# A two-layer hybrid decoder step: coarse and fine GLA products together, attention of the prompt in pairs of query blocks

## The reference, cut to what matters

```python
def layer(x, ...):
    h = rmsnorm(x, g_pre)
    (c_x, c_b, c_c, c_z, g_q, g_k, g_v, g_lr, g_z,
     s_q, s_k, s_v, s_z, m_q, m_z) = split_cols(h @ w_in)
    # A: short gated conv
    # B: GLA, 4 heads of 64: S_t = diag(a_t) S_{t-1} + k_t^T v_t, o_t = q_t S_t
    # C: sliding-window attention, window 128, rotary, a learned sink per head
    # D: cross-attention into 256 memory tokens
    mix = jnp.concatenate([a_out, b_out, c_out, d_out], axis=-1) @ w_out
    return x + rmsnorm(mix, g_post)

def memory_attention(q, mk, mv):
    s = jnp.einsum('blhd,bmhd->bhlm', q, mk) * (hd ** -0.5)
    p = jax.nn.softmax(s, axis=-1)
    return jnp.einsum('bhlm,bmhd->blhd', p, mv)
```

## Time and profile before

| | |
|---|---|
| median of 3 runs | 2365.94 us (2365.74 to 2366.8) |
| profiled execution | 2365.44 us |
| its span, first to last instruction | 2363.6 us |
| TensorE busy, matmuls | 2325.7 us, 14532 records |
| TensorE busy, weight loads | 1845.8 us |
| VectorE busy | 1369.8 us |
| ScalarE busy | 918.0 us |
| GpSimd busy | 108.2 us |
| mean granted clock of TensorE | 0.999 |

### The profile page before, as it was taken

How to read it: one execution, slowest core, us unless ns; L and a number is a source line. 1 busy time by engine, 2 the same in 40 slices (tenths; PEclk the granted TensorE clock), 3 DMA queues, 4 the chain that set the end, 5 groups by cost and what they waited for, 6 DMA issues and landing times.

```text
span 2363.6 us, 40015 instructions
## 1 busy us (share of the span) xinstructions
PE 2325.7 (98%) x14532; PEld 1845.8 (78%) x14532; DVE 1369.8 (58%) x3346; ACT 918.0 (39%) x2111; POOL 108.2 (5%) x179
## 2 busy tenths in 40 slices
PE   8999999999999999999999999999999999999998
PEld 4677777787788888878877777777878888787877
DVE  4566746565456765655536767365644676555443
ACT  4444324344434333344434543153434443233331
POOL 1000000001000000000000000000100000000000
PEclk9999999999999999999999999999999999999999
DMA  7110212244210122223331111132340113142132
GB/s 242 28 54 21 62 36 63 58 157 131 71 46 20 42 65 75 67 65 125 135 90 36 28 45 46 50 94 92 131 122 20 53 29 74 25 108 60 47 117 80
DMA packets 230557, 172.12 MB, mean 73 GB/s; under 512 B 56886, under 2 KB 206908, under 8 KB 230332
## 3 DMA queue, kind: packets, MB, share of 16 engines
q1 hardware_dynamic: 226100, 154.78, 22.8%
q10 hardware_dynamic: 4264, 14.78, 1.8%
HBM read 136.60 MB, written 21.93 MB: 67 GB/s over the span
## 4 chain that ended last, share of the span: by engine, by line
PE 95%; DVE 2%; issue 1%; ACT 1%; DMA 1%; ACTq 0%; SPq 0%; DVEq 0%; POOL 0%; POOLq 0%
PE bank L1725 53%; PE bank L2749 16%; PE bank L1820 3%; PE bank L2020 3%; PE bank L1978 3%; PE bank L1965 2%; PE bank L1804 2%; PE bank L1168 1%; PE bank L1797 1%; PE bank L1866 1%; PE bank L1962 1%; PE bank L2765 1%; PE bank L1860 1%; PE bank L1772 1%; PE bank L2010 1%
## 5 line engine op out<-in xcount | busy, mean ns | idle before, releaser
L1725 PE MATMUL bank<-h_hi,w_hi 128*128 128x512 f32 (+3 forms) x2160 | 484.5, 361 | 11.3 <-DVEq L2290 4.1
L1725 PE MATMUL bank<-h_lo,w_hi 128*128 128x512 f32 (+3 forms) x2160 | 488.7, 363 | 1.8
L1725 PE MATMUL bank<-h_hi,w_lo 128*128 128x512 f32 (+2 forms) x2080 | 468.2, 362 | 1.5
L1725 PEld LDWEIGHTS bank<-h_hi,w_hi 128*128 128x128 f32 (+1 forms) x2160 | 354.0, 186 | 89.4 <-issue 31.6
L1725 PEld LDWEIGHTS bank<-h_lo,w_hi 128*128 128x128 f32 (+1 forms) x2160 | 351.1, 185 | 73.6 <-issue 15.4
L1725 PEld LDWEIGHTS bank<-h_hi,w_lo 128*128 128x128 f32 x2080 | 343.5, 188 | 69.0 <-issue 16.2
L2749 PE MATMUL bank<-scr_r,tb_r 128*128 128x512 f32 x816 | 195.1, 395 | 2.1 <-ACT scr_r L2089 1.6
L2749 PEld LDWEIGHTS bank<-scr_r,tb_r 128*128 128x128 f32 x816 | 151.7, 188 | 36.8 <-issue 3.4
L2070 ACT ACTIVATE tb<-bank 128x512 f32<-128x512 f32 (+1 forms) x140 | 71.2, 508 | 192.8 <-PE bank L1725 186.6
L2229 ACT ACTIVATE scr<-bank 128x512 f32<-128x512 f32 x132 | 77.9, 590 | 170.3 <-PE bank L1978 169.0
L2428 DVE COPY_PREDICATED scr<-level_mask,bank 128x128 f32<-128x128 uint8 (+1 forms) x332 | 116.7, 351 | 45.6 <-PE bank L1820 26.9
(11 more groups left out here) (289 smaller groups left out, 3117.3 us busy)
## 6 DMA issues: line engine op xcount, KB each, us to landing
w_raw<-in_w_in SPq DMA_DIRECT2D x96, 512.0 KB, 3.7
out<-scr SPq DMA_DIRECT2D x32, 512.0 KB, 2.7
scr<-in_w_out SPq DMA_DIRECT2D x16, 512.0 KB, 4.9
w_raw<-in_w_out SPq DMA_DIRECT2D x16, 512.0 KB, 3.5
scr<-in_x_prompt SPq DMA_DIRECT2D x16, 512.0 KB, 3.7
scr<-out SPq DMA_DIRECT2D x16, 512.0 KB, 3.3
rot<-out ACTq DMA_DIRECT2D x12, 512.0 KB, 3.7
mix_t<-in_x_prompt ACTq DMA_DIRECT2D x8, 512.0 KB, 13.8
```

Source lines behind the costliest of these rows:

```text
L1725: m = mm(bank[b][0:m_w, 0:c1 - c0], w[:, slot, k, 0:m_w], h[:, k, c0:c1], start=it["piece"] == 0 and k == 0, stop=it["piece"] == 2 and k = ...
```

## The change

Two things. In B, `gla_g` and `gla_f` of a chunk are placed as one (both sets of banks must be free), `gla_t` stands ahead of them; the level-64 products write all 128 rows; and `gla_o` does the two products with `a` first where fine products, a score or a value visit stood last on TensorE. In C and D, items cover two blocks (`PAIRS` = 2 per step): score writes 512 columns of banks 6 and 7, `turn` fills banks 2 and 3, `value` one bank (4 for the first pair, 5 for the second). C now scales and masks in place in PSUM, and its banks too are held until the exponential. There is one buffer for the probabilities and one for their transposes, so the exponential of the second pair waits until the first pair's transposes have read them. The order of a step's items is score, score, turn, value, turn, value.

```diff
-ATT_P = layout([("p0", ST), ("p1", ST), ("pt0", ST), ("pt1", ST)])
+PAIRS = ST // CH // 2
+ATT_P = layout([("p", 2 * ST), ("pt", 2 * ST)])
...
+def keeps_banks(soft):
+    return soft["step"]["unit"] == "D" or soft["step"]["st"] != "s"
...
@@ work(s), B
+                    if c % 2 == 0:
+                        out.append(item("gla_t", [6], step=s, c=c))
                     out.append(item("gla_g", [4, 5], step=s, c=c))
                     out.append(item("gla_f", [2, 3], step=s, c=c))
-                    if c % 2 == 0:
-                        out.append(item("gla_t", [6], step=s, c=c))
@@ work(s), C and D
+            for c in range(PAIRS) if not sample else ():
+                out.append(item("score", [6, 7], step=s, c=c))
+            for c in range(PAIRS) if not sample else ():
+                out.append(item("turn", [2, 3], step=s, c=c))
+                out.append(item("value", [4 + c], step=s, c=c, j=0))
...
@@ emit(it)
+        if kind == "gla_o":
+            it["columns_first"] = it["step"]["st"] != "s" and last_on_pe[0] in ("gla_f", "score", "value")
+        if kind in ON_PE:
+            last_on_pe[0] = kind
...
@@ the loop over queues
-        def rested(it):
+        def rested(it, after=None):
+            if it["kind"] == "gla_g":
+                return max(ready(it), ready(after)) + safe
...
         emit(it)
+        if it["kind"] == "gla_g":
+            emit(queue.pop(0))
...
@@ on_tensor, gla_g
-                        rows = v if 2 * v == w else w
                         for h, hp in enumerate(heads):
-                            last[h] = mm(compact(coarse_of(h, n)[0:rows], v), x[hp, 0:rows], pairs(x[hp], v)[:, :, 1, :],
+                            last[h] = mm(compact(coarse_of(h, n), v), x[hp], pairs(x[hp], v)[:, :, 1, :],
                                          start=True, stop=True)
@@ on_tensor, gla_o
+                    if first:
+                        pe.wait_ge(attn_done, it["seq"] + 1)
+                        pe.wait_ge(coarse_done, it["seq"] + 1)
+                        for h in range(2):
+                            mm(bank[7][HD * h:HD * h + HD, 0:w], v[:, HD * h:HD * h + HD], a[0:w, h, :],
+                               start=True, stop=False, skip_group_check=True)
+                        mm(bank[7][:, 0:w], gla_state[:, g, :], qb, start=False, stop=True, skip_group_check=True)
+                        m = mm(bank[7][:, P:2 * P], kd, v, start=True, stop=True, skip_group_check=True)
...
@@ on_tensor, score
+                            for i in range(2):
+                                blk = 2 * c + i
+                                ql = q[hp, CH * blk:CH * blk + CH]
+                                dst = bank[6 + h][:, 256 * i:256 * i + 256]
...
@@ on_tensor, value
+                            for j in range(2):
+                                for i in range(2):
...
+                                    o = 4 * P * j + (2 * h + i) * P
+                                    m = mm(out[:, CH * j:CH * j + CH], v, pt[:, o:o + P], start=i == 0, stop=i == 1)
@@ on_scalar, soft
+                    if not sample and it["c"] > 0:
+                        turn_read(act, s, it["c"] - 1)
...
+                        for x in range(4):
+                            h, i = x // 2, x % 2
+                            m = fn(p[:, 256 * x:256 * x + 256], bank[6 + h][:, 256 * i:256 * i + 256], ACT.Exp, bias=z[:, 4 + x:5 + x],
+                                   scale=1.0 if unit == "C" else HD ** -0.5, accum_out=z[:, 12 + x:13 + x])
                         m.then_inc(exp_done, 1)
+                        act.drain().then_inc(bank_free[6], 1)
+                        act.drain().then_inc(bank_free[7], 1)
@@ on_scalar, turn
+                        fn(pt.rearrange("p (b n) -> p b n", b=2), psum[:, 2:4, :], ACT.Copy).then_inc(bank_free[2], 1)
+                        act.drain().then_inc(bank_free[3], 1)
@@ on_vector, score of C
+                            at = [psum[:, 6:8, 256 * i:256 * i + 256] for i in range(2)]
...
+                                link(stt(at[i], at[i], scale, mask.to_broadcast([P, 2, 256]), ALU.mult, ALU.add))
```

More of the change, by code:

```diff
@@ L286, in place @@
         elif k == "gla_g":
-            p = run("PE", 0.33 if small else 1.12, self.needs(it))
+            p = run("PE", 0.33 if small else 0.88, self.needs(it))
             q = p if small else run("ACT", 0.7, p)
@@ L291, in place @@
         elif k == "gla_f":
-            p = run("PE", 0.49 if small else 1.33, self.needs(it))
+            p = run("PE", 0.49 if small else 1.22, self.needs(it))
             at[("attn", n, c)] = q = run("DVE", 1.1 if small else 2.15, p)
@@ L300, in place @@
         elif k == "gla_o":
-            p = run("PE", 0.35 if small else 1.08, self.needs(it))
+            p = run("PE", 0.35 if small else 0.8 if it["columns_first"] else 0.93, self.needs(it))
             at[("o", n, c)] = q = run("ACT", 0.25 if small else 0.3, p)
@@ L379 @@
 TABLES_AT = 2
+ON_PE = ("proj", "gate", "rope_k", "cache_t", "score", "turn", "value", "value_part", "gla_g", "gla_f", "gla_t", "gla_kv", "gla_s",
+         "gla_o", "gla_sq", "gla_norm", "conv_out", "swa_out")
 STATS = 4
 PART_OF = {"turn": ("soft", "scale"), "fac_prod": ("fac_exp",), "gla_norm": ("spread",)}
-PART_US = {"soft": 2.3, "scale": 1.1, "fac_exp": 1.1, "spread": 0.5, "held": 1.3}
+PART_US = {"soft": 3.5, "scale": 1.4, "fac_exp": 1.1, "spread": 0.5, "held": 2.2}
 ROWS = {"A": (0, 1, 2, 3), "B": (0, 1, 2, 3), "C": (0, 1, 2, 3), "D": (0, 3)}
@@ L568, in emit @@
         if kind == "score":
-            while sum(x["kind"] in ("soft", "scale") for _, _, x in parts) >= STATS - 1:
+            it["no"] = n_scores[0]
+            n_scores[0] += 1
+            while any(x["kind"] in ("soft", "scale") and x["of"]["no"] <= it["no"] - STATS for _, _, x in parts):
                 emit_part("soft", "scale")
@@ L572, in emit @@
             while ("scale", n, c) not in placed:
-                emit_part("soft", "scale")
+                emit(parts.pop(next(i for i, x in enumerate(parts) if x[2]["kind"] in ("soft", "scale") and not behind_turn(x[2])))[2])
         elif kind == "fac_prod":
@@ L624, in emit_part, with behind_turn @@
         emit(parts.pop(next(i for i, x in enumerate(parts) if x[2]["kind"] in kinds))[2])
+    def behind_turn(soft):
+        if soft["kind"] != "soft" or soft["step"]["st"] == "s" or soft["c"] == 0:
+            return False
+        return ("turn", soft["step"]["n"], soft["c"] - 1) not in placed
     def emit_parts():
@@ L707, in ready @@
         part = {"turn": ("scale", n, c), "fac_prod": ("fac_exp", n, it.get("i", 0)), "gla_norm": ("spread", n, 0)}.get(kind)
-        held = [when + PART_US["held"] for when, _, x in parts if x["kind"] == "soft" and x["step"]["unit"] == "D"
+        held = [float("inf") if behind_turn(x) else when + PART_US["held"] for when, _, x in parts if x["kind"] == "soft" and keeps_banks(x)
                 and set(x["of"]["bank_list"]) & set(banks_of(it))]
@@ L777, in plan_units @@
             choice.clear()
-        if m and not bank_held(m):
-            choice.append((rested(m), 1, main))
-        if side and not bank_held(side[0]):
-            choice.append((rested(side[0]), 2, side))
+        for rank, q in ((1, main if m else []), (2, side)):
+            if q and not any(bank_held(x) for x in q[:2 if q[0]["kind"] == "gla_g" else 1]):
+                choice.append((rested(*q[:2]), rank, q))
         if p:
@@ L1493, in last_o, with probs_of, turn_read @@
             return max(x["seq"] for x in items if x["kind"] == "gla_o" and x["step"] is s)
-        def par(it):
-            return "0" if it["step"]["st"] == "s" else str(it["c"] % 2)
+        def probs_of(s, name):
+            return area(lay_of(s), name + "0" if s["st"] == "s" else name)
+        def turn_read(eng, s, c):
+            for b, use in att_uses[("turn", s["n"], c)].items():
+                eng.wait_ge(bank_full[b], use + 1)
         gates = {pt["step"]["n"]: x["inst"] for x in items if x["kind"] == "evict" and x["role"] == "z"
@@ L2541, in on_vector @@
                     lay = lay_of(s)
[L2542 removed]
+                    p = probs_of(s, "p")
                     z = stat[:, it["seq"] % STATS]
                     scale = HD ** -0.5
[L2545 to L2551 removed]
+                    for b in it["banks"]:
+                        filled(dve, it, b)
                     if unit == "C":
```

221 lines of the change are left out of this document (106 added, 115 removed).

## The result

The changed kernel took **2383.61 us** (2381.17 to 2386.21) where the kernel before took 2366.37 on the same chip: a ratio of 1.007 [1.0055, 1.0085], so 0.7% slower, a small loss but clear of the noise. I had forecast 2297 and a range up to 2329. The profiled execution took 2381.17 us, 15.7 more than that of before.

A forecast was written before the change was run, and what follows sets the result against it. The prediction took TensorE, busy 98% of the span at full clock, as the bound. From 2365.4 us it took 38 for attention and 32 for GLA and added 1.5 for stops: 2297 us, range 2280 to 2329.

The forecast's parts named there:

- What bounds the kernel now: Whole kernel: TensorE, busy 98% of the span at full clock, sets the time as the sum of what it streams.
- The change, GLA: Steps of B: 2.0 us less each, 32 us over 16 steps; 6 us without shape gain and columns-first.
- as long as nothing else becomes late: Whole kernel: condition under which an edit is worth what it takes from TensorE's streamed sum.
- So eight more records cost 0.47 ... I use the measured merge: Attention value visits: a second block adds 0.47 us, not 0.80, making 1.27 us a pair.
- Score ... 0.83 + 0.46 = 1.29: Attention score visits: two blocks in one visit cost 1.29 us, the second block adding 0.46.
- Transposes: Attention pairs: eight square transposes cost 0.88 us alone, nothing gained and up to 0.05 lost.
- I allow 1.5 us in all for that, bounds 0 and 20: Attention steps: TensorE stops when waiting exponentials delay projection evictions and fill both projection banks; 1.5 us in all.
- cover runs out: Attention steps: TensorE stops 1 us in each of 32 steps, 2329 us, or only 16, 2313 us; chance 0.12.
- My count of cover: Step of D: softmax chain some 17 us against 22 us of TensorE work, so covered by 5 us.
- Wide loads: Level-64 products in GLA: loading 128 weight columns for 64 costs 14 us and the shape gain, 2322 us; chance 0.07.
- Slower: Attention steps: the pair's softmax chain, not TensorE, sets each step; at 3 us a step, 2393 us; chance 0.04.

The follow-up runs named there:

- e4: The kernel before with the GLA part of the change alone: 2356.0 us, 0.9953 of the kernel before.
- e1: The changed kernel with value products ordered block, head, half of the keys, instead of head, block, half: 2358.64 us, 0.9967 of the kernel before.
- e3: The changed kernel with the value order of e1 and the score order of e2 together: 2342.88 us, 0.9893 of the kernel before.
- e2: The changed kernel with score products ordered block, then head, instead of head, then block: 2370.87 us, 1.0012 of the kernel before.
- e12: e9 with 76 transposes, results unread, ahead of waiting transposes and values in the second prompt step of C1, both passes with samples: 2324.04 us.
- e7: e3 with the second score of a C step in banks 4 and 7 instead of 6 and 7: 2329.79 us, 0.9842 of the kernel before.
- e9: e3 with the second score of a C step in banks 4 and 5, and one more planner condition on sample items: 2326.79 us.
- e8: e3 with value products ordered six records of head 0, six of head 1, then two and two: 2357.87 us, measured in one execution.

## Why the prediction was wrong, step by step

Two of the signs that the prediction named as proof against it came: a score visit of two blocks at over 1.5 us (1.84 for C), and gaps of TensorE over 1 us in steps of C.

**"What bounds the kernel now"** held as to the engine: the chain that ended last lies on TensorE for 95% before and after. But "the sum of what TensorE streams" left out its waits and its clock.

**"The change, GLA"** held in its own visits: 32.4 us less for 32, coarse to fine 0.81 (from a projection) and 0.72 (from `gla_t`) for 0.87 with its entry, column part 0.37. What failed is the condition "as long as nothing else becomes late", taken as met: 33 us less in these visits were 10.6 us less of time in e4.

**"So eight more records cost 0.47 ... I use the measured merge"** is the step that turned the sign. The row was right, but it is a row of two items in the order 4, 4, 4, 4, and the diff's loops (heads outside, blocks inside) give 8, 8. The price was 0.44 a visit more, 1.72 for 1.27: 28 us by visit sums, 25.0 in the kernel's time (e1). Without it and its like in the score of C the kernel is 1.1% faster than before (e3). I had counted the records and not read their order, though the loops stood in the diff. The Trainium skill (TensorEngine Tiling (Array Packing), Tiling Modes, Key Properties) says that different tiles can execute weight loads and products in parallel. The traces agree only where the other tile's records come soon enough in the list: with eight ahead, four of them ran alone.

**"Score ... 0.83 + 0.46 = 1.29"** was taken for C and D alike. For D it was 1.26. For C, with twice as many and narrower products, it was the same failure as above: 1.84 a visit, 0.54 above my price, for 32 visits 17 us. e2 gave 13.7 of them back in the visits and 12.7 in the time; the other 3 are 0.1 a visit that I had not priced.

**"Transposes"** held: 0.88 is the median. Their sum of 62.0 us is 64 times that and two waits of 3.0.

**"I allow 1.5 us in all for that, bounds 0 and 20"** failed as a size and as a bound. TensorE's idle time grew by 26 us, and the low clock by 34 us, which costs up to 17 more. The mechanism was in the rivals: *cover runs out*, at 16 or 32 steps of 1 us. It ran out in few steps, mostly of the passes with samples: in each of these the second scores of C waited 3.5 us in one step and 1.1 in another, and in the latter's step transposes, value and a projection waited 3.0, 1.25 and 1.25 more. The price of the clock behind a wait was missing altogether. My count of cover was made in a step of D of a plain pass (448.62 on), and the step of D there has no wait over 0.3 us in the changed kernel. C frees its banks late now (the kernel before copied the scores out first), and that edit has no term in my sum.

**Rivals 2 and 3.** *Wide loads* is refuted: the level-64 products load 128 columns, and the coarse products together got faster. *Slower* named the softmax chain; slower came, but from another place, since e3 with all its waits is already faster than before.

The ledger of the profiled executions: forecast -70; value order +28; score order +14; waits of TensorE inside attention visits +16 (from 3.5 to 19.5 us, of which 9.2 at the second scores of C); the rest of attention, the slow clock and the 0.1 a score of C, +10; gate, sample and other visits +13; outside visits +5. Sum +16, and 15.7 were measured. The two terms of order are shown by e1 and e2; the others are sums over visits and waits. How much of the last three is standing and how much is clock stays open; in e12 the clock's part of one step is 4.25 us in one pass and 1.75 in the other.

## What to carry to other kernels

When small products of two tiles of the array are to run beside each other, write the loops so that the tile changes every four records or fewer, and price a merged visit from a row that has the same order, not just the same records. Before TensorE's work is made shorter, look up in each kind of step, the leanest above all, how long it will then stand for the next result, and allow for a slow clock behind such waits as well (6.8 us of it behind the wait of 3.5 us here). If banks are held longer than before, ask who uses them next: with other banks for the second score of C the kernel came out 13 us (e7) and 16 us (e9) faster than e3, though the planner's order changed with them and e7 kept the wait.

## What the runs showed of the hardware beside this

- Records of two column halves (128x64) or of two row halves (64x128) ran side by side, two in each slot of 0.11 us, while at most four records of one stood ahead of the other's first (that one starts 13 ns behind in e3). What stood further ahead took a slot alone: 8, 10 and 12 slots of 0.109 us for 16 value records in e3, e8 and the changed kernel.
- Twice the weight columns did not slow the coarse products of level 64: their loads take 188 ns each by the groups of weight loads, 131 with 64 columns in the earlier trace rows, yet coarse to fine fell from 0.95 to 0.71, with one shape fewer in it.
- One wait of 3.5 us, or waits of 1.2 and 2.0 us in a row (with two more behind), brought the granted clock down to 1.2 GHz, for 6.8 us (the changed kernel) and 13.7 or 23.9 us (e9). Not every wait did: of the kernel before's two of 2.04 us ahead of an output stage, one was followed by 3.4 us of it and one by none. Where transposes filled e9's waits, it stayed up until 997.7.
